# Queries and keys by seven half-size products, sigmoids on ScalarE, and a re-ordered end in a fused float32 kernel

## The reference, cut to what matters

```python
# first block, each of two layers (x: 256 x 1024)
proj = x @ w_in + b_in                       # 2304 columns
c_in, q, k, v, qm = split(proj)              # 512, 512, 512, 512, 256
a, gate = split(c_in); u = a * sigmoid(gate)
y = depthwise_conv(u, 31 taps) + conv_b; conv_out = silu(layer_norm(y))
# differential attention: softmax(q1 k1) - lam * softmax(q2 k2), 4 heads, times v
# memory attention: softmax(qm km) vm
x = layer_norm(ALPHA * x + mixed @ w_out)
x = layer_norm(ALPHA * x + relu(x @ w_up)**2 @ w_down)
# second block
h = rmsnorm(x) * (1 + scale) + shift         # mean of squares over the features
y_b = rmsnorm(ssd(...) * silu(z)) @ w_o_ssd
mix = (sigmoid(g_a) * y_a + sigmoid(g_b) * y_b) @ w_out
x = x + gate * rmsnorm(mix)
x = x + gate_f * rmsnorm((silu(u_gate) * u_up) @ w_ffn_out)
```

## Time and profile before

| | |
|---|---|
| median of three runs | 1367.78 us (1367.71 to 1367.79) |
| the profiled execution's own time | 1367.69 us |
| its span | 1365.9 us |
| mean granted TensorE clock | 0.998 of full speed |
| matmul records | 8501 (two for each float32 matmul, one for a turning) |

### The profile page before, as it was taken

How to read it: one execution, slowest core, us unless ns; L and a number is a source line. 1 busy time by engine, 2 the same in 40 slices (tenths; PEclk the granted TensorE clock), 3 DMA queues, 4 the chain that set the end, 5 groups by cost and what they waited for, 6 DMA issues and landing times. The chain is left out here.

```text
span 1365.9 us, 20424 instructions
## 1 busy us (share of the span) xinstructions
PE 1346.1 (99%) x8501; PEld 1195.4 (88%) x8501; DVE 904.1 (66%) x1510; ACT 389.5 (29%) x816; POOL 156.9 (11%) x147
## 2 busy tenths in 40 slices
PE   8999999999999999999999999999999999999997
PEld 7885899988888599988888888889889985999986
DVE  3865798656287498858643778765667854856653
ACT  2153333220216233331065314343322203101100
POOL 3200322030100033022020000002100100011110
PEclk9999999999999999999999999999999999999999
DMA  9631567676432167666554242127544635455450
GB/s 311 223 124 62 185 242 258 230 257 234 166 132 85 62 228 266 247 240 216 189 63 123 90 158 81 59 95 261 156 136 157 216 136 173 144 166 186 166 173 31
DMA packets 127787, 229.70 MB, mean 168 GB/s; under 512 B 7077, under 2 KB 33981, under 8 KB 127441
## 3 DMA queue, kind: packets, MB, share of 16 engines
q1 hardware_dynamic: 123338, 218.26, 47.4%
q0 software_dynamic: 3952, 9.95, 2.4%
q10 hardware_dynamic: 407, 0.20, 0.1%
HBM read 227.30 MB, written 2.15 MB: 168 GB/s over the span
## 5 line engine op out<-in xcount | busy, mean ns | idle before, releaser
L1857 PE MATMUL acc<-y,ring 128*128 128x256 f32 (+1 forms) x1344 | 247.7, 341 | 0.1
L1857 PEld LDWEIGHTS acc<-y,ring 128*128 128x128 f32 x1344 | 216.3, 191 | 24.2 <-issue 2.5
L1857 PE MATMUL acc<-x,ring 128*128 128x128 f32 (+1 forms) x960 | 160.7, 324 | 0.0
L1857 PEld LDWEIGHTS acc<-x,ring 128*128 128x128 f32 x960 | 144.7, 191 | 12.1 <-issue 1.0
L1857 PE MATMUL acc<-ring,big 128*128 128x256 f32 (+1 forms) x376 | 115.5, 454 | 0.0
L1857 PE MATMUL acc<-ring,hid 128*128 128x256 f32 (+1 forms) x364 | 98.9, 417 | 1.4 <-DVE hid L1752 1.4
L1857 PEld LDWEIGHTS acc<-ring,big 128*128 128x128 f32 x376 | 70.8, 190 | 33.1 <-issue 26.3
L1857 PEld LDWEIGHTS acc<-ring,hid 128*128 128x128 f32 x364 | 68.5, 190 | 23.1 <-issue 15.9
L838 ACT ACTIVATE ring<-ring,silc 128x512 f32<-128x512 f32 x96 | 60.1, 708 | 93.0 <-DMA ring<-in_ada_w 93.0
L1185 DVE TENSOR_TENSOR ring<-ring 128x2048 f32<-128x2048 f32 (+1 forms) x24 | 43.7, 1821 | 31.7 <-ACT ring L838 31.3
L1857 PE MATMUL acc<-ysq,ring 128*128 128x128 f32 x528 | 64.1, 276 | 0.1
(11 more groups left out here) (480 smaller groups left out, 2474.5 us busy)
## 6 DMA issues: line engine op xcount, KB each, us to landing
ring<-in_w_in SPq DMA_DIRECT2D x24, 2048.0 KB, 9.0
ring<-in_w_up SPq DMA_DIRECT2D x16, 2048.0 KB, 9.0
ring<-in_w_down SPq DMA_DIRECT2D x16, 2048.0 KB, 8.3
ring<-in_ada_w SPq DMA_DIRECT2D x12, 2048.0 KB, 13.1
ring<-in_w_ffn_in SPq DMA_DIRECT2D x22, 1024.0 KB, 7.3
ring<-in_w_out SPq DMA_DIRECT2D x6, 2048.0 KB, 8.8
ring<-in_w_o_ssd SPq DMA_DIRECT2D x4, 2048.0 KB, 8.0
ring<-in_w_ffn_out SPq DMA_DIRECT2D x4, 2048.0 KB, 8.1
```

Source lines behind the costliest of these rows:

```text
L1857: ins = pe.matmul(dst, w, m, start=start, stop=stop, is_transpose=turned, skip_group_check=True)
```

## The change

- The queries and keys of both layers are made by seven products (`head_seven`) instead of `features`. VectorE makes four token sums and two times four weight sums before the convolution, and the combinations inside it, before taps 12 and 24 (`head_combine`). ScalarE copies each first bank, adds the biases afterwards and writes the padded keys from the combined ones in SBUF.
- Two of the four value parts are made before slot 0, two in slot 0; slots 1 to 3 have none.
- Both sigmoids of the conv branch are exp(-ln(1 + exp(-x))) on ScalarE; VectorE's additions and reciprocals go.
- The squares of x are added in pairs on VectorE, so the sum over features takes 2 matmuls instead of 8; the third bias product and three of the four turnings stand before the projection; two bias banks are emptied by VectorE.
- GpSimd's token sums for z wait for the latents' and attention's last reads instead of `cb_full`.
- In the second half of the SSD output and of the last product, m7 goes to the second half of the bank `pv_z`. VectorE finishes the low tokens' quarters from m1, m2, m3, m5 and m6 (`low_tokens`), and the high ones afterwards (`high_tokens`).
- The last scaling and the output go by token tiles, with a sum of squares for each.
- Several semaphores are merged, with the same waits (`dve_begun`, `pe_begun`, `act_begun`, `dve_stats`, `head_act`).

```diff
+        head_t = [flat12(t) for t in (hid[:, 0:12, :], hid[:, 12:24, :])]
+        head_flat = big[:, 24:32, :]
...
-            pt[:, 0, :, :], kiz[:, :, :], ysq[:, 6:8, :], pt[:, 1, :, :])]
+            pt[:, 0, :, :], kiz[:, :, :], st[:, :, :], pt[:, 1, :, :])]
...
             for n in range(2 * TT):
-                h, t = n // 2, n % 2
+                t, h = n // 2, n % 2
...
-            pool.wait_ge(cb_full, 1)
+            pool.wait_ge(h2_ready, DC)
+            pool.wait_ge(i_full, 8)
+            pool.wait_ge(o_full, DEPTH * STEPS + STEPS2)
...
+                steps.link(act.activation(ce, ce, ACT.Ln, bias=1.0))
+                act.activation(ce, ce, ACT.Exp, scale=-1.0).then_inc(head_act, 1)
...
+                def head_bank_copy(i):
+
+                    act.wait_ge(qa_full, 2 * l + i + 1)
+                    act.activation(head_flat[:, 6:8, :], acc[2 * i][:, :, :], ACT.Copy).then_inc(head_act, 1)
+                    act.wait_ge(q_combined, 2 * l + i + 1)
+
+                head_bank_copy(0)
+                for c in range(4):
+                    ins = biased(qT[:, c, :], qT[:, c, :], 4 + c)
+                ins.then_inc(drained, 2)
+                head_bank_copy(1)
+                for c in range(4):
+                    for m, half in enumerate((slice(0, 64), slice(64, 128))):
+                        ins = act.activation(kz[half, m, c, :], v[half, c, :], ACT.Identity, bias=pc[half, 8 + c:9 + c])
+                ins.then_inc(drained, 2)
+                bank[0] += 4
...
-                        act.activation(ce, ca, ACT.Exp, scale=-1.0).then_inc(cexp, 1)
+                        steps.link(act.activation(ce, ca, ACT.Exp, scale=-1.0))
+                        steps.link(act.activation(ce, ce, ACT.Ln, bias=1.0))
+                        act.activation(ce, ce, ACT.Exp, scale=-1.0).then_inc(head_act, 1)
...
+            def head_weight_sums(i):
+
+                m, t, base = l * LAYER_UNITS + 2 + i, head_t[i], 8 * l + 4 * i
+                w = ring[:, m % RING]
+                b11, b12, b21, b22 = w[:, 0:4, 0:Q], w[:, 0:4, Q:], w[:, 4:8, 0:Q], w[:, 4:8, Q:]
+                dve.wait_ge(loaded[m % RING], 16 * (m // RING + 1))
+                tt(t[:, 0], b12, b11, ALU.subtract).then_inc(hw_ready, 1)
+                tt(b12, b22, b12, ALU.subtract).then_inc(hw_ready, 1)
+                dve.wait_ge(hw_ready, base + 1)
+                tt(t[:, 1], b22, t[:, 0], ALU.subtract).then_inc(hw_ready, 1)
+                dve.wait_ge(hw_ready, base + 3)
+                tt(t[:, 2], b21, t[:, 1], ALU.subtract).then_inc(hw_ready, 1)
+
+            def head_combine(i, dst):
+
+                n, f = 2 * l + i, head_flat
+                by_tile = lambda ap: ap.rearrange("p (a t) -> p a t", t=H)
+                dve.wait_ge(head_act, 4 * l + i + 2)
+                dve.wait_ge(qb_full, n + 1)
+                tt(dst[:, 0:2, 0:H], by_tile(f[:, 6, :]), by_tile(acc[2 * i + 1][:, 0, :]), ALU.add)
+                steps.link(tt(f[:, 1, :], f[:, 6, :], acc[2 * i + 1][:, 1, :], ALU.add))
+                dve.wait_ge(qc_full, n + 1)
+                steps.link(tt(f[:, 2:4, :], f[:, 1:2, :].broadcast_to([P, 2, T]), scr[i][:, :, :], ALU.add))
+                tt(dst[:, 2:4, H:T], by_tile(f[:, 2, :]), by_tile(scr[i][:, 1, :]), ALU.add)
+                tt(dst[:, 2:4, 0:H], by_tile(f[:, 3, :]), by_tile(f[:, 7, :]), ALU.add)
+                dve.wait_ge(filled, l * LAYER_ACCS + HEAD_ACCS + 6 + 2 * i)
+                tt(dst[:, 0:2, H:T], by_tile(f[:, 2, :]), by_tile(pv_z[:, 0, :]), ALU.add).then_inc(q_combined, 1)
+
+            def first_bias_back(t):
...
-                dve.wait_ge(drained, done + 4)
-                steps.link(ts(ce, ce, 1.0, None, ALU.add))
-                steps.link(dve.reciprocal(ce, ce))
+                a11, a12, a21, a22 = x[:, 0:4, 0:H], x[:, 4:8, 0:H], x[:, 0:4, H:T], x[:, 4:8, H:T]
+                tt(sx[:, 0], a21, a22, ALU.add).then_inc(hx_ready, 1)
+                tt(sx[:, 2], a11, a21, ALU.subtract).then_inc(hx_ready, 1)
+                dve.wait_ge(hx_ready, 4 * l + 1)
+                tt(sx[:, 1], sx[:, 0], a11, ALU.subtract).then_inc(hx_ready, 1)
+                dve.wait_ge(hx_ready, 4 * l + 3)
+                tt(sx[:, 3], a12, sx[:, 1], ALU.subtract).then_inc(hx_ready, 1)
                 if l == 0:
-                    dve.wait_ge(warm_ready, 1)
+                    dve.wait_ge(bias_out, 16)
+                for i in range(2):
+                    head_weight_sums(i)
+                dve.wait_ge(head_act, 4 * l + 1)
...
+                    if tap == 12:
+                        head_combine(0, qT)
+                    if tap == 24:
+                        head_combine(1, v)
...
+            first_bias_back(1)
+            dve.wait_ge(xsq_ready, 2)
+            tt(ysq[:, 0:2, :], ysq[:, 0:2, :], ysq[:, 2:4, :], ALU.add).then_inc(xsq_sum, 1)
+            dve.wait_ge(xsq_ready, 4)
+            tt(ysq[:, 4:6, :], ysq[:, 4:6, :], ysq[:, 6:8, :], ALU.add).then_inc(xsq_sum, 1)
+            dve.wait_ge(xsq_sum, 2)
+            tt(ysq[:, 0:2, :], ysq[:, 0:2, :], ysq[:, 4:6, :], ALU.add).then_inc(xsq_sum, 1)
...
+            def high_tokens(k, c21, c22):
+
+                s, before = (k + 1) % 2, TAIL_G + k
+                dve.wait_ge(mz_full, before + 1)
+                steps.link(tt(quads[:, 2, :], quads[:, 2, :], pv_z[:, 1, :], ALU.add))
+                tt(c22, quads[:, 2, :].rearrange("p (a t) -> p a t", a=2), scr[s][:, 1, :].rearrange("p (a t) -> p a t", a=2), ALU.add)\
+                    .then_inc(mc_free, 1)
+                tt(c21, quads[:, 2, :].rearrange("p (a t) -> p a t", a=2), pv_z[:, 0, :].rearrange("p (a t) -> p a t", a=2), ALU.add)\
+                    .then_inc(mz_free, 1)
...
-            combine2_quad(G_SSD + 1)
+            low_tokens(G_SSD + 1, in_quad(0), in_quad(1))
             dve.wait_ge(c_step, 2 * (TAIL_G + G_SSD + 1) + 2)
             mixed_half(1, 0)
-            combine2_last(G_SSD + 1, in_quad(4))
+            high_tokens(G_SSD + 1, in_quad(4), in_quad(5))
+            dve.wait_ge(mc_free, TAIL_G + G_SSD + 4)
             dve.wait_ge(mz_free, TAIL_G + G_SSD + 3)
...
+            low_tokens(G_DOWN + 1, down_quarter(0, 0), down_quarter(0, 1))
+            dve.wait_ge(c_step, 2 * (TAIL_G + G_DOWN + 1) + 2)
+            gained_tokens(0)
+            row_sum(0)
+            high_tokens(G_DOWN + 1, down_quarter(1, 0), down_quarter(1, 1))
+            dve.wait_ge(mc_free, TAIL_G + G_DOWN + 4)
+            dve.wait_ge(mz_free, TAIL_G + G_DOWN + 3)
+            gained_tokens(1)
+            for t in range(TT):
+                if t:
+                    row_sum(1)
+                dve.wait_ge(rdown_ready, t + 1)
+                dve.wait_ge(ygain_ready, 8)
+                for h in range(2):
...
+                def head_seven(w, i):
+
+                    t, n = head_t[i], 2 * l + i
+                    free_bank()
+                    free_bank()
+                    product(w[:, 0:4, 0:Q], x[:, 0:4, 0:H], acc[2 * i][:, 0, :], True, True)
+                    pe.wait_ge(hx_ready, 4 * (l + 1))
+                    product(w[:, 4:8, Q:], sx[:, 3], acc[2 * i][:, 1, :], False, True).then_inc(qa_full, 1)
+                    product(w[:, 4:8, 0:Q], x[:, 4:8, 0:H], acc[2 * i + 1][:, 0, :], True, True)
+                    pe.wait_ge(hw_ready, 4 * n + 3)
+                    product(t[:, 1], sx[:, 1], acc[2 * i + 1][:, 1, :], False, True).then_inc(qb_full, 1)
+                    product(t[:, 0], sx[:, 0], scr[i][:, 1, :], True, True)
+                    product(w[:, 0:4, Q:], sx[:, 2], scr[i][:, 0, :], False, True).then_inc(qc_full, 1)
+                    pe.wait_ge(hw_ready, 4 * n + 4)
+                    if i:
+                        pe.wait_ge(q_combined, n)
+                    elif l == 0:
+                        ready(2)
+                    product(t[:, 2], x[:, 4:8, H:T], pv_z[:, 0, :], True, True).then_inc(filled, 2)
...
+                value_part(vb, wv, 0, 1).then_inc(filled, 1)
+                vb = free_bank()
...
-                        value_part(vb, wv, 0, 1).then_inc(filled, 1)
-                    elif k == 1:
-                        vb = free_bank()
                         value_part(vb, wv, 1, 0)
-                    elif k == 2:
-                        value_part(vb, wv, 1, 1, range(0, DC // 2))
+                        value_part(vb, wv, 1, 1).then_inc(filled, 1)
+                        to_release[0] += 1
                     elif k == 3:
-                        value_part(vb, wv, 1, 1, range(DC // 2, DC)).then_inc(filled, 1)
-                        to_release[0] += 1
                         pe.wait_ge(conv_done, l + 1)
...
+            bias_products(2)
             pe.wait_ge(x2high_ready, DC * DEPTH)
-            mean_squares2(xsq_ready, 0, 2, ysq, DC)
-            bias_products(2)
+            mean_squares2(xsq_sum, 2, 2, ysq, 2)
+            pe.wait_ge(x2low_ready, DC * DEPTH)
+            for n in (0, 1, 3):
```

(10 more changed lines are left out.)

181 lines of the change are left out of this document (98 added, 83 removed).

## The result

The changed kernel takes 1373.44 us (1370.90 to 1374.68, five runs), before it was 1367.71 (1367.64 to 1367.79): ratio 1.0039, 95% interval 1.0026 to 1.0052. Slower, beyond the 0.2% that can be told from no change. The profiled execution took 1374.68 us, its span is 1372.9: 7.0 us more than before. Timed again beside other kernels, the unedited changed kernel took 1373.99 (1370.65 to 1374.65; 1.0040, 1.0027 to 1.0053). Its own runs lie 4 us apart, those of before 0.15.

A forecast was written before the change was run, and what follows sets the result against it. TensorE, busy 99%, was taken to bound the kernel, with VectorE short of room in layer 0. Terms +11.0 + 0.6 - 1.8 - 1.3 - 1.4 + 0.35 = +7.5 on 1367.69 gave 1375.2 us, range 1369.0 to 1379.5.

The forecast's parts named there:

- TensorE's saving: Queries and keys, both layers: seven products save TensorE 1.25 us a unit, 5.0 us for four units.
- Layer 0, VectorE: Layer 0: VectorE, free at 38.4 us, begins the convolution's taps at 55.0 instead of 48.3 and ends them at 84.3.
- contention: Layer 0 weight sums: each of GpSimd's 8 scaling operations costs VectorE about 0.35 us, 2.8 us in all.
- Layer 0, TensorE: Layer 0: TensorE waits 7.4 us for the padded keys; slot 4 starts 9.2 us late; +11.0 us with the clock.
- wait for the bank: Layer 0: TensorE's last product waits 1.0 us for the bank that the queries' combination frees.
- slots: Attention slots without value parts, both layers: TensorE waits 1.8 and 0.9 us for VectorE's weights, plus 0.4 us for resuming.
- The clock cost: Layer 0 behind the wait for the keys: the clock falls to half and costs 1.8 us, bounds 0 and 2.3.
- Layer 1: Layer 1: VectorE's sums fit its idle time, no wait before the scores, slot waits remain; -2.5 + 3.1 = +0.6 us.
- The gains behind layer 1: Second block's start -1.8 us, GpSimd's sums for z -1.3 us, half-product's own bank in the SSD output -1.4 us.
- A: Rival: layer 0 late, but without contention and at full clock, +6.1 us there; 1370.3 us in all; chance 0.20.
- B: Rival: TensorE's work alone counts, if layer 0's keys are combined before about 70.5; 1358.5 us; chance 0.12 with half-way form.
- B's half-way form: Rival: as B, but the slot waits of both layers kept, 3.1 us each; 1364.7 us; chance 0.12 together with B.

The follow-up runs named there:

- e3: Changed kernel with queries and keys of both layers computed plainly again and the values back in the slots: 1365.11 us (0.9980 of the kernel before).
- e9: Changed kernel with layer 0 plain, seven products in layer 1 alone, its last value quarter in slots 1 and 2, second sigmoids on VectorE: 1361.28 us.
- e1: Changed kernel with VectorE combining layer 0's keys before tap 16 instead of tap 24: 1366.45 us.
- e8: Changed kernel, layer 0 keys plain with values in slots, layer 1's last value quarter in slots 1 and 2, second sigmoids on VectorE, lambda loads first: 1359.93 us.
- e4: Changed kernel with GpSimd scaling x in layer 0 only after the convolution is done: 1371.63 us.
- e10: Changed kernel with lambda loads first and 14 added matmuls, their result overwritten, ahead of layer 0's first scores: 1371.54 us.
- e5: Changed kernel with the lambda vectors' loads issued ahead of the first two weight units: 1370.21 us.
- e2: Changed kernel with the last quarter of the values computed in slots 1 and 2 of both layers instead of slot 0: 1368.43 us.
- e6: Changed kernel with each layer's second sigmoid finished by VectorE's addition and reciprocal again: 1371.90 us.
- e0: The changed kernel, unedited, timed a second time: 1373.99 us.
- e7: Changed kernel with layer 0 keys combined before tap 16, last value quarter in slots 1 and 2, second sigmoids on VectorE, lambda loads first: 1364.16 us.
- e11: Changed kernel with each layer's first sigmoid finished by VectorE's addition and reciprocal again: 1379.81 us.

## Why the prediction was right, step by step

- **What bounds it.** TensorE's list and, in layer 0, VectorE's. Shown from both sides: e3 and e9 run layer 0 at the old pace without VectorE's new work, and e1 moves the end by VectorE's order alone.
- **TensorE's saving.** 1.25 us a unit predicted, 1.3 measured: 67.51 - 42.40 = 25.1 us for two, 27.7 before. Right; e8 collects it in layer 0 for one unit (slot 4 at 89.38, 90.61 in the earlier trace rows).
- **Layer 0, VectorE.** The taps began at 53.2, I had 55.0. VectorE was free 0.7 us later than in the earlier trace rows, by the lambda load; the token sums took 0.4 less; and contention took 0.9 us in front of the taps instead of 2.8, with 0.4 more inside them (e4: 1.3 in all). The term was mis-sized because I let each of GpSimd's operations cost VectorE a full turn; it was GpSimd that lost most. The Trainium skill (GPSIMD Engine Reference, Specifications) says that GpSimd shares SBUF interfaces with VectorE and contends with those of its instructions that have two SBUF inputs. The traces agree, and e4 says at what price.
- **Layer 0, TensorE.** Wait for the keys 6.8 (7.4 predicted), no wait for the bank (1.0 predicted: the combination was done at 64.97, TensorE came at 65.7), slots 1.6 and 0.75 (1.8 and 0.9). The clock cost 92.20 - 81.36 - 8.63 = 2.2 us where I took 1.8. The place of the price was right: e10 takes 1.8 of it away from e5. Whether it has to be paid varies. The Trainium skill (TensorE: Matmul & The Clock Gate, Why this matters for your kernels) says that idle gaps between bursts of matmuls bring the half clock back. This trace agrees (granted clock 0.80 over the stretch of the wait and 0.77 behind it), and e2's does not (1.00 behind 3.53 us). The prediction had one slip here: 82.6 and its own 1.73 and 6.9 give 91.2, not 91.5.
- **Layer 1.** Keys and TensorE meet as predicted: the keys stood 0.7 us ahead (0.6 predicted), no wait, and the same two slot waits (1.60 and 0.75). Right, but for the second sigmoid.
- **The step that was missing.** The prediction priced the second sigmoid's move nowhere. Behind it stood the exponentials of the last attention steps (e3, e6): 0.8 to 0.9 us a layer, 1.7 in all. It nearly made up for the 1.6 us that layer 0 was taken too high, which is why the sum came out within 0.5 us of the trace. That closeness is luck, twice over: two errors of opposite sign, and the profiled execution is the slowest of the five, with the latest lambda load of all traces. The medians say +5.7, 1.8 us less than the forecast. It was an error of the same kind as those that I looked for elsewhere: an operation put ahead of others on an engine that is 29% busy.
- **The gains behind layer 1.** -1.6, -1.4 and -1.6 against -1.8, -1.3 and -1.4, and +0.2 at the end against +0.35. All within 0.25 us.
- **The rivals.** A (1370.3) is the time of the changed kernel's fastest executions (1370.65 in e0's trace), though with a fallen clock: VectorE's early start, not the absence of contention, gives it. B, faster, needed the keys' combination before about 70.5. e1 has it at 69.3, and TensorE no longer waits for the keys; but at 1366.45 it is near B's half-way form (1364.7, with the second sigmoids' 1.7 on top) and far from its 1358.5, since the slots' waits stay.
- **Open.** How e5's spread of 3.6 us divides, with the lambda load out of the way. Two things vary in it. One is the wait for the second weight unit (1.20, 0.54 and 0 us in e5, e7 and e10). The other is the clock, whose mean over each run is on record: 0.998 in e5's two fastest runs (1368.07 and 1368.66) and 0.996 in its three slowest (1371.58 to 1371.68). As an estimate from these, 0.002 of 1370 us is up to 2.7 us. In the changed kernel's ten runs it is the same: the fastest of each five (1370.90 and 1370.65) has 0.998, the others 0.996. One run of e5, 1371.08 at 0.998, does not fit, and no experiment holds one of the two still while the other varies. What decides whether the clock falls stays open as well.

## What to carry to other kernels

Work moved from the bounding engine to one that is idle on average has to fit where it lands: two units of seven products paid in layer 1, where VectorE idled in front of them, one paid in layer 0, and a second one there made the kernel 4.2 us slower (e7 against e8, which also differ in where the values of layer 0 stand), though TensorE's list is 1.25 us shorter with it. When such work is threaded into another engine's list, place each piece by the time at which its input is there and its reader comes, not evenly, and leave the bounding engine something to do in the slots that it will now reach early. And price every operation that is put in front of others, also on the engine that seems free.

## What the runs showed of the hardware

- The granted clock fell to half at single waits of TensorE of 2.52 (e11), 3.13 (e5), 3.30 (e0), 5.83 (e11), 6.29 (e6) and 6.78 us, and at 1.04 and 2.08 us close to each other (e7), but not at 3.53 us (e2) or 1.75 us (e4). Where it fell before the scores of the changed kernel, e0 and e5, it cost 1.8 to 2.2 us. In these traces the length of the wait alone does not tell whether it falls, so one profile of a kernel with such a wait says little about its median. The mean granted clock of each run helps a little: among the profiled executions it is 0.998 or 0.999 where the clock did not fall, and 0.995 to 0.998 where it did.
- The four small lambda loads, issued behind two weight units, let VectorE go on anywhere between 32.5 (e4) and 36.4 us (the changed kernel's first profile), in kernels whose instructions are alike up to there. Before the change nothing hung on them: its five first runs lay within 0.15 us and 33 later ones within 0.63. Afterwards they lay 4 us apart. A spread that a change brings is itself a sign: the path now runs through something that varies, here a load and the clock.
- Where VectorE's tensor-tensor operations on 128x1024 met GpSimd's scaling of 128x256 in the changed kernel, VectorE's took up to 1.50 us instead of 1.22, and GpSimd's eight 11.09 us instead of 4.2.
